# Hybrid decoder trunk on one core: the narrow projection weights in two loads of adjoining columns, and the small loads behind them

## The reference

```python
h = layer_norm(x, ln_in_g, ln_in_b)
(pool_v, fq, fk, fv, ff, dq, dk, dv, iq, ik, iw, conv_in, gate) = split_columns(h @ w_in[l])
br_a = pool_mixer(pool_v, pool_w[l], pool_scale[l])
br_b = fox_attention(fq, fk, fv, ff + b_forget[l])          # 4 heads of 64
br_c = dsa_attention(dq, dk, dv, iq, ik, iw)                # shared key and value of 64, indexer
br_d = conv_module(conv_in, ...)
# four branches projected, gated by sigmoid(gate), merged, w_out, residual, layer norm, MoE, layer norm
```

## Time and profile before

| | us |
|---|---|
| median of 3 runs | 470.65 (468.97 to 470.86) |
| the profiled execution | 470.3, its span 468.6 |
| PE busy | 448.2 (96% of the span) |
| DVE, ACT, POOL busy | 251.7, 172.6, 58.3 |
| read from memory | 139.47 MB |

### The profile page before, as it was taken

How to read it: one execution, slowest core, us unless ns; L and a number is a source line. 1 busy time by engine, 2 the same in 40 slices (tenths; PEclk the granted TensorE clock), 3 DMA queues, 4 the chain that set the end, 5 groups by cost and what they waited for, 6 DMA issues and landing times.

```text
span 468.6 us, 7037 instructions
## 1 busy us (share of the span) xinstructions
PE 448.2 (96%) x2813; PEld 310.2 (66%) x2813; DVE 251.7 (54%) x526; ACT 172.6 (37%) x276; POOL 58.3 (12%) x67
## 2 busy tenths in 40 slices
PE   6999999999999999999989999999999999999790
PEld 5899999999999999988864434543444434443230
DVE  5069949989987776996781312322221313222047
ACT  5076366445575777253652111211122101101035
POOL 8954910000000000000015200000000000000000
PEclk9899999999999999999999999999999999999997
DMA  7993534533555544999957999999999999999962
GB/s 244 295 339 111 180 109 142 188 134 151 179 180 180 180 167 154 404 421 348 364 209 273 427 420 422 422 419 420 422 420 422 421 421 421 420 422 422 420 250 90
DMA packets 39215, 140.96 MB, mean 301 GB/s; under 512 B 6744, under 2 KB 10993, under 8 KB 26896
## 3 DMA queue, kind: packets, MB, share of 16 engines
q1 hardware_dynamic: 37856, 138.72, 76.1%
q10 hardware_dynamic: 752, 1.58, 1.0%
q0 software_dynamic: 576, 0.23, 0.3%
HBM read 139.47 MB, written 1.05 MB: 300 GB/s over the span
## 4 chain that ended last, share of the span: by engine, by line
PE 78%; SPq 9%; DMA 8%; DVE 3%; ACT 1%; issue 1%; DVEq 0%; ACTq 0%
PE bank L1128 20%; PE bank L1412 16%; SPq L468 9%; PE bank L1436 8%; PE bank L1038 6%; DMA ring<-in_expert_w_down_dram 6%; PE bank L1268 5%; PE bank L1009 4%; PE bank L1257 4%; PE bank L1343 2%; PE bank L1353 2%; DMA ring<-in_w_in_dram 2%; PE bank L1249 1%; PE bank L1051 1%; PE bank L1063 1%; PE bank L1160 1%
## 5 line engine op out<-in xcount | busy, mean ns | idle before, releaser
L1412 PE MATMUL bank<-ring,gates 128*64 128x512 f32 x512 | 113.5, 594 | 4.4 <-DMA ring<-in_expert_w_up_dram 2.6
L1128 PE MATMUL bank<-rounded 128*128 128x256 f32 x768 | 95.0, 284 | 0.0
L1128 PEld LDWEIGHTS bank<-rounded 128*128 128x128 f32 x768 | 92.8, 192 | 0.8 <-issue 0.7
L1412 PEld LDWEIGHTS bank<-ring,gates 128*64 128x64 f32 x512 | 35.9, 137 | 73.4 <-issue 68.1
L1436 PE MATMUL bank<-ring,gates 128*64 128x512 f32 x256 | 57.8, 597 | 0.1
L1996 DVE SCALAR_TENSOR_TENSOR gates<-gates,bank 128x512 f32<-128x512 f32 x8 | 6.0, 747 | 77.4 <-PE bank L1412 77.4
L1581 DVE TENSOR_TENSOR rounded<-ring,rounded 128x1024 fp32r<-128x1024 f32 x32 | 37.0, 1222 | 9.3 <-ACT rounded L723 9.3
L1436 PEld LDWEIGHTS bank<-ring,gates 128*64 128x64 f32 x256 | 17.2, 136 | 33.6 <-issue 29.9
L2008 DVE TENSOR_TENSOR rounded<-bank,rounded 128x512 fp32r<-128x512 f32 x16 | 11.1, 692 | 48.3 <-ACT rounded L938 39.1
L723 ACT ACTIVATE rounded<-ring 128x1024 fp32r<-128x1024 f32 x32 | 31.2, 1056 | 4.1 <-PE bank L1038 4.1
L1038 PE MATMUL bank<-rounded 128*128 128x256 f32 x240 | 29.6, 284 | 0.0
(11 more groups left out here) (286 smaller groups left out, 576.2 us busy)
## 6 DMA issues: line engine op xcount, KB each, us to landing
ring<-in_expert_w_gate_dram SPq DMA_DIRECT2D x32, 1024.0 KB, 17.2
ring<-in_expert_w_up_dram SPq DMA_DIRECT2D x32, 1024.0 KB, 20.0
ring<-in_expert_w_down_dram SPq DMA_DIRECT2D x32, 1024.0 KB, 20.1
ring<-in_w_in_dram SPq DMA_DIRECT2D x10, 2048.0 KB, 7.8
ring<-in_w_branch_dram SPq DMA_DIRECT2D x2, 2048.0 KB, 7.9
ring<-in_w_out_dram SPq DMA_DIRECT2D x2, 2048.0 KB, 10.3
ring<-in_w_in_dram SPq DMA_DIRECT2D x3, 1024.0 KB, 15.8
ring<-in_w_in_dram SPq DMA_DIRECT2D x1, 1280.0 KB, 9.4
```

The costliest lines, as they stand in the source:

```text
L1128: last = pe.matmul(bank[:, b, c * T:(c + 1) * T], w[wpart][:, k, at:at + P], hT_part[hpart][:, k, :], start=(k == 0 and hpart == wpart), s ...
L1412: done = pe.matmul(bank[CAP * e:CAP * e + CAP, part // 2, :], xg[:, FC * h + k, c:c + CAP], w[:, e, k * HALF:(k + 1) * HALF], start=(h == ...
```

## The change

The two groups of columns that lie side by side become one transfer each: `s_idx` is iq, ik, iw (324 columns), `s_dsa` is ff, dq, dk, dv (388 columns). So iw is now in slot 0 and dk in slot 1. DVE copies iw and ff behind dv in slot 1, so that misc finds its 72 columns side by side, and signals `s_mw`. The unit of ik and dk takes its columns from two slots: per k one matmul of 64 columns to partitions 0 to 63 and one to partitions 64 to 127. ACT, before it overwrites slot 0 with the rounded hT, and PE, before misc, wait for the copies. The second unit of PE now waits for `s_dsa` (before, the third did). POOL asks for the vector rows and gate biases no longer at its start but behind its constants, and behind a wait for `s_dsa`; its other ten transfers stand behind them.

```diff
@@ -286,6 +286,7 @@
+        s_mw = sem("narrow_weights_side_by_side")
@@ -385,7 +386,7 @@
-        FRONT = {"s_idx": (0, 2), "s_dsa": (1, 4), "s_fox": (2, 1), "s_val": (3, 2), "s_conv": (4, 1),
+        FRONT = {"s_idx": (0, 1), "s_dsa": (1, 1), "s_fox": (2, 1), "s_val": (3, 2), "s_conv": (4, 1),
@@ -432,7 +433,8 @@
-        IDXC, DSAC = BW + 2 * DH, BW + DH + 2 * NH
+        IDXC, LOADC = BW + DH + NH, NH + BW + 2 * DH
+        DSAC, DKC, DVC = LOADC + 2 * NH, NH + BW, NH + BW + DH
@@ -472,16 +474,9 @@
-            d = slot("s_idx", IDXC)
-            n = BW + DH
-            sp.dma_start(d[:, :, 0:n], w_in[:, :, col["iq"]:col["iq"] + n]).then_inc(s_slot[0], 16)
-            sp.dma_start(d[:, :, n:n + DH], w_in[:, :, col["dk"]:col["dk"] + DH]).then_inc(s_slot[0], 16)
-            d = slot("s_dsa", DSAC)
-            at = 0
-            for name in ("dq", "dv", "iw", "ff"):
-                n = sizes[name]
-                sp.dma_start(d[:, :, at:at + n], w_in[:, :, col[name]:col[name] + n]).then_inc(s_slot[1], 16)
-                at += n
+            sp.dma_start(slot("s_idx", IDXC), w_in[:, :, col["iq"]:col["iq"] + IDXC]).then_inc(s_slot[0], 16)
+            sp.dma_start(slot("s_dsa", DSAC)[:, :, 0:LOADC], w_in[:, :, col["ff"]:col["ff"] + LOADC])\
+                .then_inc(s_slot[1], 16)
@@ -560,9 +555,6 @@
-            for r, src in vec_src[2:]:
-                pool.dma_start(vrows[r:r + src.shape[0], :], src).then_inc(s_vr, 16)
-            pool.dma_start(grows, a["b_gate"][0].rearrange("(r p) -> r p", p=P)).then_inc(s_vr, 16)
             link(pool.memset(causal[:, :], 0.0))
@@ -589,6 +581,10 @@
+            loaded(pool, "s_dsa")
+            for r, src in vec_src[2:]:
+                pool.dma_start(vrows[r:r + src.shape[0], :], src).then_inc(s_vr, 16)
+            pool.dma_start(grows, a["b_gate"][0].rearrange("(r p) -> r p", p=P)).then_inc(s_vr, 16)
             pw = a["pool_w"][0]
@@ -685,6 +681,7 @@
             act.wait_ge(s_unit, 2)
+            act.wait_ge(s_mw, 1)
             act.wait_ge(s_hTd, TB * KC // 2)
@@ -1067,14 +1064,21 @@
             by_channel(w, 0, BW, True)
-            by_channel(w, BW, 2 * DH)
             loaded(pe, "s_dsa")
-            w = slot("s_dsa", DSAC)
-            by_token(w, BW, DH + 2 * NH)
+            w2 = slot("s_dsa", DSAC)
+            o = start_unit()
+            for k in range(KC):
+                for r, part, c0 in ((0, w, BW), (DH, w2, DKC)):
+                    last = pe.matmul(o[r:r + DH, 0, :], part[:, k, c0:c0 + DH], hT[:, k, :],
+                                     start=(k == 0), stop=(k == KC - 1))
+            last.then_inc(s_unit, 1)
+            w = w2
+            pe.wait_ge(s_mw, 1)
+            by_token(w, DVC, DH + 2 * NH)
@@
-            by_channel(w, 0, BW)
+            by_channel(w, NH, BW)
@@ -1528,6 +1532,11 @@
+            loaded(dve, "s_idx")
+            loaded(dve, "s_dsa")
+            w2 = slot("s_dsa", DSAC)
+            dve.tensor_copy(w2[:, :, LOADC:LOADC + NH], slot("s_idx", IDXC)[:, :, BW + DH:IDXC])
+            dve.tensor_copy(w2[:, :, LOADC + NH:DSAC], w2[:, :, 0:NH]).then_inc(s_mw, 1)
             dve.wait_ge(s_hThi, 1)
```

## The result

| us | before | after |
|---|---|---|
| median (4 runs each) | 469.81 (468.93 to 470.86) | 474.48 (473.76 to 475.02) |
| profiled execution, its span | 470.3, 468.6 | 473.76, 472.0 |

The ratio is 1.0106 [1.0081, 1.0131]: 1.1% slower, in the forecast's own range (474.4, 473.0 to 475.6). The lines of the kernel after are shifted: L1006 is L1009 of before, L1541 is L1532, L1546 is L1537, L1035 is L1038, and hn's product and sum are L581 and L582. L1072 is the new ik/dk unit, L1015 misc.

What follows compares the result with a forecast made beforehand. PE's unbroken work from 12 to 37 us was taken to bound the kernel. Start -1.1, clock -1.5, stops +5.2, second low clock +1.5 made +4.1 on 470.3: 474.4, range 467.9 to 475.6 (forecast's own 473.0 to 475.6).

Steps and rivals of the forecast that it cites:

- What bounds the kernel: From 12 to 37 us PE works alone, so each microsecond it starts earlier or is stopped reaches the end undiminished.
- Edit 1: At PE's first unit: one 1296 KB load lands at 11.1 to 11.2, PE starts at 11.15 instead of 12.26: -1.1.
- The clock held: Behind PE's start: without the idle microsecond ahead of it PE's clock does not fall: -1.5 (bound 0).
- Edits 2 and 3: ik/dk unit in column halves runs at the old price; DVE's two copies and the waits for them cost nothing: 0.
- rival E: In the ik/dk unit the column halves do not overlap: +3.6 before the fox unit, some 471 to 474; chance 0.03.
- Edit 4: Fewer, merged loads: earlier fox weights alone give 0; the second load lands at 15.9, upper bound 18.2.
- Rival C: Second load at 17.9 or later, hn after 28.65, two or three quarters through first: 467.7 to 468.2; chance 0.2.
- Edit 5: POOL's transfers behind its wait move hn from 20.18 to 26.65, where it alternates with DVE's fox rests: +5.2.
- The stops: In the first fox unit PE waits 2.4 for the third quarter and 2.8 for the fourth: +5.2.
- The low clock: Behind the two fox-unit stops PE's clock falls a second time: +1.5 (bounds 0 and +1.7).
- The rule that I had weighed: Behind the fox-unit stops: the clock falls only after a wholly idle stretch, so 0 instead of 1.5, time 472.9.
- Sum: Whole kernel: -1.1 - 1.5 + 0 + 5.2 + 1.5 = +4.1 against the profiled 470.3, giving 474.4.

Runs made afterwards that it cites:

- experiment 1: The changed kernel with only POOL's order undone, vector rows asked for at its start and no wait for the second load: 467.98, ratio 0.9972.
- experiment 7: The changed kernel with hn held until DVE's first fox quarter is done: 471.03, ratio 1.0037.
- experiment 3: The changed kernel with hn held back until DVE has all four fox quarters: 471.91, ratio 1.0052.
- experiment 5: The kernel before with POOL's move alone, its vector rows behind the constants and a wait for s_dsa: 475.75, ratio 1.0142.
- experiment 9: The changed kernel with each of hn's four operations cut into two of 512 elements: 471.37, ratio 1.004.
- experiment 4: The changed kernel with 13 and 18 identity transposes on PE ahead of its waits for the third and fourth quarter: 472.17, ratio 1.006.
- experiments 6 and 10: 6: changed kernel, hn ahead of POOL's eighteen transfers: 479.35, ratio 1.0211. 10: that plus POOL's s_val rests held for DVE's second indexer score: 471.06, ratio 1.0038.

## Why the prediction was right

**What bounds the kernel.** Right. All of the difference is in the span's first 52 us and reaches the end undiminished.

**Edit 1, start.** Predicted -1.1, measured 12.26 - 10.92 = **-1.34**. The load landed 8.8 us behind its issue at 1.72, at 10.5, not at 11.1 to 11.2. Much of that is this one execution: in the eight experiments that carry the new load the same transfer took 8.9 to 9.7, and PE's first unit began at 10.8 to 11.4, so -1.1 was as good a figure as -1.3. In the profiled execution PE waited 0.3 for ACT's hT, so the input set the start, near the bound of -1.3. The clock held: **-1.5**, as predicted, against a profiled execution in the slower third of before's runs. That is an advantage of the sum's base, not of every run. Against the median of before's 33 runs the change costs 474.48 - 468.84 = 5.6 us.

**Edits 2 and 3.** Predicted 0, measured **+0.2**: from 10.92 to 34.14 PE takes 23.22, where before took 36.75 - 12.26 - 1.50 = 22.99. The unit in column halves took 3.63 for 8 x 0.444 = 3.55, and the one behind it is longer too (3.72 in experiment 1, 3.52 in before). The halves do overlap, so rival E is out. DVE's copies ended at 15.1, well ahead.

**Edit 4.** The second load landed 12.5 behind its issue at 2.19, at 14.7, ahead of the 15.5 to 18.2 that I had given (in the experiments it took up to 13.4). The two loads among the issues of the kernel after:
```profile
ring<-in_w_in_dram SPq DMA_DIRECT2D x1, 1552.0 KB, 12.5
ring<-in_w_in_dram SPq DMA_DIRECT2D x1, 1296.0 KB, 8.8
```
The parameters were asked for early, at 10.54:
```profile
10.54 0.35 ACTq L659 DMA_DIRECT2D lnp<-in_ln_in_g_dram  x1
```
I had set this at 11.8, behind ACT's hT pieces: wrong, the issue needs only the landing, and ACT's last pieces run beside it. It made no difference. Until 13.9 none of the parameters' packets had moved, and from 12.5 up to 14.7 38 of theirs stood against 437 of SP's queue; then the two went one for one, 85 to 85 up to 16. Rival C needed the load at 17.9 or later and had no ground left. The rule by which it would have held (the Trainium skill, DMA: Bandwidth & Descriptors: an engine drains a whole packet of descriptors before it changes queue) isn't borne out by these counts either.

The price that rival C put on a late hn would not have held. C gave 467.7 to 468.2 for an hn that starts after 28.65. In experiment 7 it started at 29.28 and every quarter was in time, and the kernel took 471.03; in experiment 3 it started at 32.03, at 471.91. The step that fails there is that POOL beside DVE's small operations costs nothing: through ACT's rounding and POOL's rests it costs PE 2.4 us. And in experiment 5, with hn from 31.09, 2.5 behind the start of the first quarter, all four quarters were slow, where C lets two or three through.

**Edit 5, order of POOL.** POOL's eighteen issues took 25.77 - 15.02 = 10.75, as predicted (4.25 + 6.50). hn began at 25.77 instead of 26.65, for the load was 1.2 earlier and the wait's release 0.3 later. This 0.9 cost nothing: POOL's first operation had to wait for DVE's L1541 in either case, and got its turn at 27.5, where I had put it.

**The stops.** Predicted 5.2, measured **4.5**. The mechanism is as forecast: turns of one whole instruction, third and fourth quarter late, two stops. I had the period at 1.15 + 2.36 = 3.51; it is 3.30: the ends of the operations follow each other by 1.08 (DVE) and 2.22 (POOL), both a little less than the 1.15 and 2.36 that they take alone. Quarters due at 38.0 and 41.5 came at 37.4 and 40.7. PE wanted them at 35.6 and 38.2, late by 1.9 and 2.6. The Trainium skill (SBUF — State Buffer, Who interferes with whom) describes the port pair that the two engines share as an exclusive lock for the whole instruction. The trace agrees, and the period follows the length of POOL's operation (3.3 and 2.2 in experiment 9).

**The low clock.** Predicted +1.5, measured **+1.5** in the profiled execution (experiment 4). It is no constant: experiment 5 paid 2.5, above my bound of +1.7. I had leaned on a stretch with transposes in the earlier trace rows; here PE was wholly idle in 36 to 37 and 39 to 40, and the clock read 0.75 and then 0.50 from 41 on. The rule that I had weighed (the Trainium skill, TensorE: Matmul & The Clock Gate, part 1: only a wholly idle stretch lowers the clock) gave 0 in my reading. The clock fell all the same, behind two stops of 1.7 and 2.3 us idle with 1 us of work between them, so this trace does not bear that 0 out. Nor do, where it fell behind transposes and 1.58 us idle, though only in a third of the runs.

**Sum.** -1.34 - 1.50 + 0.23 + 6.03 = **+3.4**, where 6.03 is the fox and fk stretch, from PE's arrival at 34.14 to 51.88, less the 11.71 of before: 4.5 and 1.5. Predicted +4.1: the stops were sized 0.7 too large and the start 0.2 too small, and the halves had been left out. The median is 0.7 above the profiled execution, which makes up for it: that 474.4 is met within 0.1 is partly luck.

## What to carry to other kernels

A work item off the critical path has a place in time, and to move it counts as an edit: ask which shared resource it meets there. Here eighteen harmless DMA issues and a wait that costs nothing pushed four POOL operations of 2.4 us into the stretch in which PE lives on DVE's results. Load merges and later transfers are worth having (467.98 and 468.21 against 468.84), if hn keeps its early place; and if VectorE must run beside GpSimd, short GpSimd operations shorten each turn (2.2 us for 3.3 in experiment 9).

## What the runs showed of the hardware that I had not expected

- VectorE can be kept out for far longer than one operation: 19.92 us and 13.52 us under eight gap-free GpSimd operations (experiments 6 and 10), though it took turns with the four of hn and, in the kernel after, with the same eight run as closely.
- Size and the number of inputs do not protect a VectorE operation: one of 8 elements with one input took 2.35 instead of 0.17 (experiment 3). The maximum searches were untouched.
- A VectorE quarter begun at 28.62 took 3.38 us though GpSimd only issued transfers up to 31.09 (experiment 5); in the kernel after, such issues up to 25.77 did nothing of the kind to L1541, begun at 25.23.
- TensorE's clock after the same idle microsecond falls in some executions and not in others: two groups of runs of one unchanged kernel, 1.9 us apart by their medians. And what it costs once it has fallen varies, 1.5 us in the kernel after and 2.5 in experiment 5 for the same 78 records.
